# Recurrent heads: the first of seven level matmuls with 64 weight columns instead of 128, and a plain copy of its result instead of a masked one

## What is computed

```
step(state, chunk):
    diff   = b[t] - b[s]                  # b: running sum of log decays, per channel
    scores = sum_d q[t,d] * k[s,d] * exp(diff[t,s,d])      for s <= t
    o      = scores @ v  +  (q * exp(b)) @ state
    state  = exp(b_last) * state + (k * exp(b_last - b))^T @ v
```

## Time and profile before

| | |
|---|---|
| median of 3 runs | 3841.64 us |
| lowest, highest | 3841.49, 3853.27 us |
| the profiled execution: time, span | 3853.37, 3851.6 us |
| its mean granted TensorE clock | 0.956 of full |
| TensorE matmuls busy | 3520.7 us, 91% of the span |
| VectorE busy | 2110.2 us, 55% |
| ScalarE busy | 1552.9 us, 40% |
| GpSimd busy | 1372.5 us, 36% |

### The profile page before, as it was taken

The page is one execution under the profiler, slowest core; times in us unless marked ns, Lnnn a source line. Parts: engine busy times, 40 slices in busy tenths (PEclk is TensorE's granted clock), DMA queues, the critical chain, the costliest instruction groups (busy, mean ns, idle before and its releaser), DMA issues.

```text
span 3851.6 us, 62125 instructions
## 1 busy us (share of the span) xinstructions
PE 3520.7 (91%) x18848; PEld 2866.5 (74%) x18848; DVE 2110.2 (55%) x5638; ACT 1552.9 (40%) x3145; POOL 1372.5 (36%) x1636
## 2 busy tenths in 40 slices
PE   8999999999999999999998999979887999798878
PEld 6887887666777878877665879867775798677747
DVE  5655555666255555655766253266665332666653
ACT  5434443444245444443444242245453222454532
POOL 6544553332624554553333612122213112222131
PEclk9999999999999999999999999999998999899979
DMA  4100012110221001012111222111111421111124
GB/s 140 34 28 28 28 34 58 36 41 26 96 91 43 29 28 33 27 33 56 41 41 37 93 83 66 57 38 35 37 30 60 156 72 58 37 35 37 30 60 156
DMA packets 217956, 206.80 MB, mean 54 GB/s; under 512 B 17948, under 2 KB 185004, under 8 KB 216668
## 3 DMA queue, kind: packets, MB, share of 16 engines
q1 hardware_dynamic: 197536, 137.80, 12.8%
q0 software_dynamic: 12208, 47.03, 3.5%
q10 hardware_dynamic: 7920, 18.45, 1.5%
HBM read 148.30 MB, written 37.01 MB: 48 GB/s over the span
## 4 chain that ended last, share of the span: by engine, by line
PE 73%; DVE 10%; issue 7%; ACT 5%; DMA 2%; POOL 1%; DVEq 1%; SPq 0%; ACTq 0%; POOLq 0%
PE banks L923 24%; PE banks L1203 8%; PE banks L1088 5%; PE banks L1140 5%; PE banks L959 5%; PE banks L1314 4%; PE banks L1262 3%; PE banks L1112 3%; PE banks L1034 2%; PE banks L1044 2%; PE banks L1165 2%; PE banks L1056 1%; PE banks L1240 1%; DVE BB L1934 1%; PE banks L1241 1%
## 5 line engine op out<-in xcount | busy, mean ns | idle before, releaser
L923 PE MATMUL banks<-H,whi 128*128 128x512 f32 x3200 | 1055.3, 411 | 14.4 <-POOL wlo L614 12.6
L923 PEld LDWEIGHTS banks<-H,whi 128*128 128x128 f32 x3200 | 581.0, 191 | 188.3 <-issue 68.2
L923 PE MATMUL banks<-H,wlo 128*128 128x512 f32 x1600 | 636.5, 398 | 0.0
L613 POOL CAST whi<-raw 128x1024 fp32r<-128x1024 f32 x150 | 162.1, 1081 | 1220.6 <-PE banks L923 557.4
L1203 PE MATMUL banks<-H,whi 128*128 128x346 f32 (+1 forms) x1536 | 384.0, 333 | 9.9 <-DVEq L408 8.0
L614 POOL TENSOR_TENSOR wlo<-raw,whi 128x1024 fp32r<-128x1024 f32 x150 | 363.7, 2425 | 12.1
L923 PEld LDWEIGHTS banks<-H,wlo 128*128 128x128 f32 x1600 | 305.5, 191 | 71.2
L1963 DVE COPY_PREDICATED AT<-lvl,banks 128x64 f32<-128x64 int32 x896 | 222.0, 248 | 173.0 <-PE banks L966 134.8
L2230 DVE TENSOR_SCALAR_CACHE_REDUCE SP<-banks 128x346 f32<-128x346 f32 (+3 forms) x432 | 201.6, 513 | 197.9 <-PE banks L1241 196.5
L1203 PEld LDWEIGHTS banks<-H,whi 128*128 128x128 f32 x1536 | 275.3, 195 | 20.2 <-issue 14.0
L1538 ACT ACTIVATE SM<-SM,stt 128x256 f32<-128x256 f32 (+1 forms) x256 | 124.7, 488 | 329.1 <-DVE stt L2076 329.1
(11 more groups left out here) (286 smaller groups left out, 7216.5 us busy)
## 6 DMA issues: line engine op xcount, KB each, us to landing
raw<-in_w_in SPq DMA_DIRECT2D x148, 512.0 KB, 3.9
raw<-in_w_out SPq DMA_DIRECT2D x64, 256.0 KB, 2.7
raw<-in_w_out SPq DMA_DIRECT2D x18, 512.0 KB, 3.3
XT<-x_resident POOLq DMA_DIRECT2D x16, 512.0 KB, 3.9
x_resident<-XT POOLq DMA_DIRECT2D x16, 512.0 KB, 2.9
XB<-x_resident POOLq DMA_DIRECT2D x16, 512.0 KB, 4.7
out_x<-XB POOLq DMA_DIRECT2D x16, 512.0 KB, 5.4
x_resident<-XB POOLq DMA_DIRECT2D x16, 512.0 KB, 6.1
```

The costliest lines, as they stand in the source:

```text
L923: last = nc.tensor.matmul(bank(half if bk is None else bk), w[:, slot, k, :], H[:, part, a:a + 512], start=k == 0 and n == 0, stop=k == DT ...
```

## The change

For level 64, TensorE takes as weights only the 64 early tokens (64 columns of `EX`) and writes a 64 by 64 result to partitions 0 to 63 of bank 2. VectorE copies these with `tensor_copy` to the block of `AT` that belongs to them, without the mask. The loops over `n` have one turn at `hs = 64`. The other six levels, the counts and all semaphores stay.

```
                         for li, hs in enumerate(LEVELS):
-                            late = EX[:, j, 1 + li, c2 * P:c2 * P + P].rearrange("p (n w s) -> p n w s", w=2, s=hs)[:, :, 1, :]
-                            nc.tensor.matmul(psum[2][:, li * 64:li * 64 + 64].rearrange("p (n s) -> p n s", s=hs),
-                                             EX[:, j, 1 + li, c2 * P:c2 * P + P], late, start=True, stop=True)
+                            e = EX[:, j, 1 + li, c2 * P:c2 * P + P].rearrange("p (n w s) -> p n w s", w=2, s=hs)
+                            if hs >= 64:
+                                for n in range(64 // hs):
+                                    nc.tensor.matmul(psum[2][2 * hs * n:2 * hs * n + hs, li * 64 + hs * n:li * 64 + hs * n + hs],
+                                                     e[:, n, 0, :], e[:, n, 1, :], start=True, stop=True)
+                            else:
+                                nc.tensor.matmul(psum[2][:, li * 64:li * 64 + 64].rearrange("p (n s) -> p n s", s=hs),
+                                                 EX[:, j, 1 + li, c2 * P:c2 * P + P], e[:, :, 1, :], start=True, stop=True)
...
                     for li, hs in enumerate(LEVELS):
                         o = AT[:, c % 2, :].rearrange("p (n w s) -> p n w s", w=2, s=hs)[:, :, 1, :]
                         own.n += 1
-                        V.copy_predicated(o, lvl[:, li * 64:li * 64 + 64].rearrange("p (n s) -> p n s", s=hs),
-                                          psum[2][:, li * 64:li * 64 + 64].rearrange("p (n s) -> p n s", s=hs)).then_inc(own.sem, 1)
+                        if hs >= 64:
+                            for n in range(64 // hs):
+                                last = V.tensor_copy(AT[2 * hs * n:2 * hs * n + hs, c % 2, 2 * hs * n + hs:2 * hs * n + 2 * hs],
+                                                     psum[2][2 * hs * n:2 * hs * n + hs, li * 64 + hs * n:li * 64 + hs * n + hs])
+                            last.then_inc(own.sem, 1)
+                        else:
+                            V.copy_predicated(o, lvl[:, li * 64:li * 64 + 64].rearrange("p (n s) -> p n s", s=hs),
+                                              psum[2][:, li * 64:li * 64 + 64].rearrange("p (n s) -> p n s", s=hs)).then_inc(own.sem, 1)
```

## The result

The changed kernel takes 3874.12 us (median of 6 runs, 3869.62 to 3880.88) against 3843.53 us (3841.49 to 3853.27, 6 runs) before: a ratio of 1.0076, 95% interval 1.0062 to 1.0091. It is **30.6 us slower**, by the interval 24 to 35. The forecast was 24 us slower, the range 3831 to 3878.

The account below looks back on a forecast made before the run. The prediction took TensorE to set the pace in 100 of 128 slots. At 0.24 us more each, +24 us on the median of 3841.6 gave 3865.6 us, VectorE counted as 0; the range was 3831 to 3878.

Parts of the forecast that it names:

- The switch, both ways: TensorE's level part: array waits going into and out of the 64 column passes, loads exposed; 0.24 us more a slot.
- the sum: Per slot: 0.10 emptying, 0.056 first load, two passes of 0.056, 0.20 way out; 0.47 us replacing two 0.112 passes.
- Which slots pay: TensorE sets the pace in 100 of 128 slots, which pay; the 28 where VectorE is late count 0.
- VectorE at 0: Plain instead of masked copy of 64 columns on VectorE: counted 0, between a loss of 2 and a gain of 2 us.
- the clock at a change of heads: TensorE idles about 2 us for the head norm and its clock may fall; allowed 6 us either way.
- No wait, as in rows 8: Rival, chance 0.2: 64 column loads stay hidden, like 16 column ones; 0.11 us saved in 86 slots, 3832 us.
- One side waits only: Rival, chance 0.12: only the way in or out of the narrow passes waits; 0.05 to 0.09 us lost a slot, about 3848 us.
- More than the 100 slots pay: Rival, chance 0.08: VectorE delayed too in slots 3 and 6 (31 us), or more low-clock stretches (up to 6); 3873 to 3879 us.

Follow-up runs that it names:

- two tiles: Against the kernel before, all seven levels in tiles of 64 weight columns, the lower six as two matmuls each on array halves, plain level 64 copy: 3817.16 us, ratio 0.9916.

## Why the prediction was right

**The switch, both ways.** It held: both loads wait, the narrow one 0.10 us and the full one about as long, and both stand in the open. In the slot it came to 0.225 us, not 0.24. The distance of full passes is 0.112 us in the level part, as I had it. But two terms of the sum were too long, and it was luck that they nearly cancel. Counted from where the state update lets the next pass start, the second pass of level 32 starts 0.282 us later before and 0.512 with the change (means of 112 slots); my terms give 0.335 and 0.58. Before, the second pass of level 64 comes 0.058 us behind the first and not 0.112, and behind the switch the full passes too come sooner than my terms have them. The difference, 0.230, is what I needed. The runs with one matmul twice and with 72 columns show that it is the switch, not the narrow matmul.

**Which slots pay.** 100 of 128; shown by the run that is narrow in slots 3 and 6 alone. 100 x 0.225 = 22.5 us against the 24 forecast.

**VectorE at 0.** Held, with the copy alone at a ratio of 0.9999 (0.9987 to 1.0010). That no slot of a last head waits for VectorE held before, and failed in slot 6 with the change, by 2.4 us in both layers together.

**What I sized wrong.** Most likely the clock at a change of heads. I gave it 6 us to either side with a mean of zero. In the profiles it was 7.1 us to one side at the changes of heads, less 2.3 us beside them: none of 14 passes at full clock with the change, 3 to 7 in the kernels in which the switch is missing or stands in slots 3 and 6 alone. The measured 30.6 is 22.5 and some 8 more, of which the clock is the largest part that a trace shows. With an interval of 24 to 35 the forecast's 24 lies at the edge of what was measured.

**The rivals.** "No wait, as in rows 8" is out; the row it rested on is of another type and width. "One side waits only" is out by the load side's timeline. "More than the 100 slots pay" was wrong in its first half. Its second half, more stretches at the low clock, is what the profile of the change has. Its number, 31 us, was met by the median, but it came from 128 paying slots, which is not what happened.

The Trainium skill's rule on the change of tiling mode ("TensorEngine Tiling (Array Packing)", Tiling Modes) agrees with the float32 matmuls here, at 64 and at 32 columns. Taken with its list, it disagrees with the 16 column float32r passes of the earlier trace rows, and there the measurement decides.

## What to carry to other kernels

Before narrowing one matmul in a run of full ones, look in the trace for a place where the weight tile changes and count both edges: in float32 here they cost 0.23 us more than the columns saved. Group narrow work so that the edges are paid once, and use the other half of the array; the two together turned a loss of 31 us into a gain of 30. Then check what bounds each step of the loop, since an added wait is free in slots that another engine ends, and a saved one gains nothing there.

## What was not expected of the hardware

- Two passes with 64 columns among their like cost 0.12 us together, where two full ones take 0.22.
- In the kernel before, the second pass of the level part starts 0.058 us after the first, the others at a distance of 0.112, so a load of 72 columns shortened a slot by 0.05 us only.
- Adding three matmuls to a head brought a standstill of 2.8 to 3.1 us at three of four turns of TensorE's loop, with 165 packets of instructions in place of 138.
- In two tiles, passes with 32 moving columns start every 0.03 us.
- A multiply of 128x512 on VectorE took 2.86 us in one execution and 0.78 in another at the same place, and TensorE waited for it.
